# The front of a two-block transformer: x loaded transposed, modulation quarters 2 to 9 as running sums on VectorE, position tables loaded later

## The chip, the cores and the metric

The kernel runs on one core of a Trainium2 chip as one program. The metric is the device time of one execution in microseconds (us), and the median of the runs is quoted. All data are float32.

## The reference

Three transformer blocks run over one sequence of 1024 tokens with 1024 channels. The change lies in the front, the first stage. There the reference computes, for each block, modulation values from a conditioning vector, and for the first block the projection of the modulated tokens:

```
c_act = silu(c)                                   # c is 1 x 1024
mod = c_act @ ada_w[i] + ada_b[i]                 # 1024 x 6144, i = 0, 1; block 3 has w_mod, b_mod and its own c
sh1, sc1, g1, sh2, sc2, g2 = split(mod, 6)
h = x * (1 + sc1) + sh1                           # x is 1024 x 1024
qkv = (h @ w_qkv).reshape(S, 3, 16, 64)           # 1024 x 3072
q = qkv[:, 0] * 64 ** -0.5
```

Neighbourhood attention over q, k, v follows, with a bias table indexed by the distance of the tokens (na_rpb), then the other stages. The front has to deliver q, k and v, all three rows of modulation values (18432 in all), and the spread position tables.

## The kernel before

The front is the function of that name. D = S = 1024, and a matrix of 1024 rows is eight blocks of 128 partitions.

**Quarters and chunks.** The three modulation matrices have 3 x 6144 columns, cut into nine pieces of 2048 columns, called quarters. Only quarter 1 (q = 0 in the code: sh1 and sc1 of the first block) is needed in the front itself; quarters 2 to 9 are written to memory for later stages. A quarter of weights is 8 MB and comes in four chunks of 2 MB. For each chunk TensorE makes a partial sum (partial, L370): for two k and four column groups a matmul with a column of the activated c, spread over 32 columns, as the stationary operand, and 512 columns of weights as the moving one. The four groups lie in four bands of 32 columns of the array and run side by side, and float32 matmuls appear twice in the trace, as two passes. After the fourth chunk VectorE adds the bias to the sum in PSUM (add_row, L478) and POOL stores the row (L352).

**x.** SP loads x by rows into the tile v. TensorE turns it, 64 transposes into PSUM (turn_x, L359), and VectorE and ScalarE copy the results to hT (L432, L446).

**From quarter 1 to h.** When all four chunks of quarter 1 are summed, ScalarE copies the sums to part, four small matmuls turn them into columns (columns, L385), VectorE adds the bias and 1 and multiplies hT in place, eight instructions of 128x1024 (L476).

**Items.** The projection is 48 items (L391) of eight matmuls with 512 moving columns, for six blocks c of 512 weight columns. The blocks of weights (2 MB, L321) lie in two buffers. For c below 4 an item gives 128 columns of q or k, transposed, for half of the tokens; then come the items of v (L407), which are written to the tile v. Four PSUM banks take the items in turn; even items are copied out by VectorE, odd ones by ScalarE. Item n waits until item n - 4 is copied.

**Order.** All of it is written out by hand, as one list per engine. After the items n with n % 3 of 1 or 2 TensorE does one chunk's partial sum (chunk_after): 32 chunks among 48 items. SP is the only queue for large loads and works in order; a chunk's load waits until the chunk two before it is summed (L311).

```
for m in range(FIRST, CHUNKS):
    if m in (12, 17, 22, 28):
        load_weights(2 + (12, 17, 22, 28).index(m))
    load_chunk(m)
```

**POOL** zeroes a table in memory, writes eight shifted copies of the position biases into it and spreads it with 16 more DMAs (L342 to L348), at the start of the program; then it stores the rows of the quarters, and the stage ends when the last store has landed. A barrier of all engines stands between the front and the attention (na in tile names, L531 its first load).

Of the kernel before, what the change touches and what calls it, by code (L numbers as in the profile page):

```python
# [16 lines left out]
P = 128  # L17
# [3 lines left out]
ALU = mybir.AluOpType  # L21
# [4 lines left out]
S = 1024  # L26
# [225 lines left out]
def front(nc, name, a, x, w, mods, table, spread_table, qT, kT, v):  # L252
# [6 lines left out]
    KC, CW, QW, FIRST = D // P, 512, 2048, 4  # L259
    QUARTERS = len(mods) * (6 * D // QW)  # L260
    CHUNKS, ITEMS = 4 * QUARTERS, 48
    H, R, C = a["na_rpb"].shape[1:]
    wv = w.rearrange("(c p) n -> p c n", p=P)
    x_rows = rows(x)
    flat_table = table.rearrange("c h r k -> (c h r k)").rearrange("(p n) -> p n", p=P)
    with Stage(nc, name) as st:
        ident, sel = st.sb("ident", [P, P]), st.sb("sel", [P, 4])
        ccol, cact = st.sb("ccol", [P, 2, KC]), st.sb("cact", [P, 2, KC])
        bcol, col = st.sb("bcol", [P, 2 * KC]), st.sb("col", [P, 2 * KC])
        mw, brow = st.sb("mw", [P, 2, 2, QW]), st.sb("brow", [P, 2, CW])  # L270
# [4 lines left out]
        turn = [st.ps(f"turn{e}", [P, 512]) for e in range(2)]  # L275
        acc = [st.ps(f"acc{e}", [P, 512]) for e in range(4)]
        mp, ms = st.ps("mp", [P, 512]), st.ps("ms", [P, 512])
        id_in, c_in, b_in, act_done = (st.sem(n) for n in ("id_in", "c_in", "b_in", "act_done"))
# [3 lines left out]
        mw_in, brow_in = [st.sem(f"mw_in{j}") for j in range(2)], [st.sem(f"brow_in{j}") for j in range(2)]  # L282
        turned, evac = st.sem("turned"), [st.sem(f"evac{e}") for e in range(2)]
        part_done, part_cp, sum_done, cols_done, h_ready = (st.sem(n) for n in ("part_done", "part_cp", "sum_done", "cols_done", "h_ready"))
        mm_done, mm_cp = st.sem("mm_done"), [st.sem(f"mm_cp{e}") for e in range(2)]
# [8 lines left out]
        def chunk_buffer(m):  # L294
            if m < FIRST:
                return (qT, kT)[m // 2][:, 4 * (m % 2):4 * (m % 2) + 4].rearrange("p a n -> p (a n)").rearrange("p (i n) -> p i n", i=2)
            return mw[:, m % 2]

        def chunk_after(n):

            return FIRST + 2 * (n // 3) + n % 3 - 1 if n % 3 else None
# [2806 lines left out]
```

## Time and profile before

| | before |
|---|---|
| median of 3 runs | 4301.48 us (4300.26 to 4303.33) |
| profiled execution, span | 4301.6 us |
| TensorE busy, whole span | 3568.8 us (83%) |
| VectorE busy, whole span | 1470.4 us (34%) |
| front: first instruction to the next stage's first load | 0.4 to 454.6 us |
| DMA, whole span | 842 MB, mean 196 GB/s |

The profiled execution has a span of 4301.6 us from its first to its last instruction, 0.1 us beside the median of the runs; no other time of that execution is given. PE is TensorE (PEld its weight loads), DVE VectorE, ACT ScalarE, POOL GpSimd, SP the queue of loads. In a timeline a row gives start, duration, engine and line, the operation, output<-inputs, the shape and a count; in brackets stands how long the engine had been idle and for whom. In the view by stretches a row gives, after the limits and the length, the busy us of PE, PEld, DVE, ACT and POOL with their instructions, the granted TensorE clock as a share of full speed, the busy share of the DMA engines and what they moved. In the groups by line a row ends with the busy us, the mean ns of one instruction and the idle time before them. The DMA issues end with the median us from issue to landing.

### The profile page before, as it was taken

What the parts mean: (1) busy time and instruction counts of PE and PEld (TensorE: products, weight loads), DVE (VectorE), ACT (ScalarE), POOL (GpSimd) and SP (SyncE); (2) the same over time, 40 slices, a digit from 0 to 9 for tenths busy, and PEclk for the clock granted to TensorE, in tenths of its full rate; (3) what the DMA queues carried; (4) which work ended last, traced back from release to release, by engine and by line L of the source; (5) the groups of instructions that cost most, each with busy time, mean ns of one, the idle gap of its engine ahead of it and who ended that gap; (6) DMA issues with size and microseconds to landing.
All of it is one profiled execution on the core that took longest, in us unless ns stands there. A gap on an engine that the chain in (4) does not pass through costs nothing. (4 is left out here: it accounts for less than half of the span.)

```text
span 4301.6 us, 49622 instructions
## 1 busy us (share of the span) xinstructions
PE 3568.8 (83%) x19450; PEld 1989.7 (46%) x19450; DVE 1470.4 (34%) x2609; ACT 873.4 (20%) x1883; POOL 242.1 (6%) x277
## 2 busy tenths in 40 slices
PE   7999889479999598999874999986999476929970
PEld 3333555334444244777542444433557374527650
DVE  1000455400000484666452000004426762631116
ACT  0000450001111123555200110102335311001111
POOL 1000200100000010000002000000000000010002
PEclk9999999589999798999986999997999787959995
DMA  8555312099999420000314999955210403129964
GB/s 311 203 201 200 123 57 108 25 389 427 426 424 391 173 84 6 1 2 2 125 64 155 426 426 427 420 217 203 98 51 1 149 3 123 69 64 420 420 272 149
DMA packets 175632, 842.34 MB, mean 196 GB/s; under 512 B 53199, under 2 KB 60111, under 8 KB 129330
## 3 DMA queue, kind: packets, MB, share of 16 engines
q1 hardware_dynamic: 140306, 735.20, 42.6%
q0 software_dynamic: 21856, 58.35, 3.8%
q10 hardware_dynamic: 13248, 45.67, 2.6%
q8 instruction: 158, 2.59, 0.2%
q14 instruction: 64, 0.52, 0.0%
HBM read 758.39 MB, written 97.20 MB: 199 GB/s over the span
## 5 line engine op out<-in xcount | busy, mean ns | idle before, releaser
L403 PE MATMUL front_acc<-front_hT,front_wt 128*128 128x512 f32 x512 | 226.7, 599 | 2.2 <-DMA front_wt<-in_na_w_qkv 2.2
L1238 PE MATMUL n_acc<-n_wt,n_hT 128*128 128x512 f32 (+2 forms) x512 | 191.1, 530 | 0.7 <-ACT n_hT L1278 0.7
L201 DVE TENSOR_REDUCE gqa_top<-gqa_scores 128x1 f32<-128x1024 f32 x128 | 150.8, 1220 | 101.8 <-PE gqa_scores L149 101.8
L232 ACT ACTIVATE gqa_probs<-gqa_scores,gqa_top 128x1024 f32<-128x1024 f32 x128 | 142.5, 1113 | 169.0 <-DVE gqa_top L201 169.0
L2160 PE MATMUL m1x_gp<-m1x_w,m1x_xT 128*128 128x512 f32 (+1 forms) x512 | 172.1, 600 | 1.5 <-issue 0.7
L2160 PE MATMUL m0x_gp<-m0x_w,m0x_xT 128*128 128x512 f32 (+1 forms) x512 | 171.9, 599 | 1.5 <-DVE m0x_xT L2236 0.7
L2185 PE MATMUL m0x_yp<-m0x_w,m0x_hidT 128*128 128x512 f32 (+1 forms) x512 | 169.3, 594 | 2.1 <-ACT m0x_hidT L2246 2.1
L2185 PE MATMUL m1x_yp<-m1x_w,m1x_hidT 128*128 128x512 f32 (+1 forms) x512 | 169.3, 594 | 2.1 <-ACT m1x_hidT L2246 2.1
L2160 PE MATMUL m0x_up<-m0x_w,m0x_xT 128*128 128x512 f32 (+1 forms) x512 | 168.8, 592 | 0.0
L2160 PE MATMUL m1x_up<-m1x_w,m1x_xT 128*128 128x512 f32 (+1 forms) x512 | 168.8, 592 | 0.0
L936 PE MATMUL n_acc<-n_wt,n_hT 128*128 128x512 f32 x384 | 168.0, 597 | 0.7 <-ACT n_hT L954 0.7
L403 PEld LDWEIGHTS front_acc<-front_hT,front_wt 128*128 128x128 f32 x512 | 96.1, 191 | 132.3 <-issue 128.7
L139 PE MATMUL gqa_turn<-gqa_ident,gqa_probs 128*128 128x128 f32 x1024 | 140.4, 281 | 0.1
L139 PEld LDWEIGHTS gqa_turn<-gqa_ident,gqa_probs 128*128 128x128 f32 x1024 | 110.4, 141 | 59.6 <-issue 59.6
L149 PE MATMUL gqa_scores<-k1T,q1T 64*128 64x512 f32 x512 | 131.9, 630 | 5.8 <-DMA gqa_ident<-in_ident 3.3
L1238 PEld LDWEIGHTS n_acc<-n_wt,n_hT 128*128 128x128 f32 x512 | 97.8, 194 | 83.0 <-issue 77.9
L1730 PE MATMUL n_acc<-n_wt,mixT 128*128 128x512 f32 x256 | 114.1, 605 | 15.1 <-DMA n_wt<-in_w_out 15.1
L168 PE MATMUL gqa_out<-gqa_probsT,v 128*64 128x128 f32 x2048 | 125.9, 276 | 0.8 <-ACT gqa_probsT L228 0.8
L1730 PE MATMUL n_acc<-n_wt,o1T 128*128 128x512 f32 x256 | 114.1, 605 | 15.0 <-DMA n_wt<-in_gqa_w_o 15.0
L1730 PE MATMUL n_acc<-n_wt,q0T 128*128 128x512 f32 x256 | 113.7, 604 | 15.2 <-DMA n_wt<-in_na_w_o 15.2
L2300 DVE TENSOR_TENSOR m1x_hid<-m1x_sg,m1x_up 128x512 f32<-128x512 f32 x24 | 16.5, 687 | 321.2 <-PE m1x_up L2160 321.2
L2300 DVE TENSOR_TENSOR m0x_hid<-m0x_sg,m0x_up 128x512 f32<-128x512 f32 x24 | 16.5, 687 | 320.7 <-PE m0x_up L2160 320.7
(612 smaller groups left out, 5529.9 us busy)
## 6 DMA issues: line engine op xcount, KB each, us to landing
m0x_w<-in_moe_w_gate SPq DMA_DIRECT2D x32, 2048.0 KB, 32.8
m0x_w<-in_moe_w_up SPq DMA_DIRECT2D x32, 2048.0 KB, 32.3
m0x_w<-in_moe_w_down SPq DMA_DIRECT2D x32, 2048.0 KB, 33.2
m1x_w<-in_moe_w_gate SPq DMA_DIRECT2D x32, 2048.0 KB, 33.0
m1x_w<-in_moe_w_up SPq DMA_DIRECT2D x32, 2048.0 KB, 31.9
m1x_w<-in_moe_w_down SPq DMA_DIRECT2D x32, 2048.0 KB, 33.4
front_mw<-in_ada_w SPq DMA_DIRECT2D x20, 2048.0 KB, 7.4
m2x_w<-in_moe_w_gate SPq DMA_DIRECT2D x32, 1024.0 KB, 32.2
```

What stands on the lines that cost most here:

```text
L139: last = pe.transpose(turn[f % TURN][:, i * P:(i + 1) * P], src, ident[:, :])
L149: last = pe.matmul(scores[h][:, c * 512:(c + 1) * 512], qT[half, j, t * P:(t + 1) * P], kT[half, 2 * j // SHARE, c * 512:(c + 1) * 512], s ...
L168: pe.matmul(out[h * HEAD:(h + 1) * HEAD, 0:P], v[:, k, kv * HEAD:(kv + 1) * HEAD], probsT[:, n % 2, h, k], start=k == 0, stop=k == TILES - 1)
L201: dve.tensor_reduce(top[:, n % 2, h:h + 1], scores[h][:, :], AX.X, ALU.max, negate=True).then_inc(max_ready, 1)
L232: act.activation(probs[:, n % 2, h], scores[h][:, :], ACT.Exp, bias=top[:, n % 2, h:h + 1], accum_out=total[:, n % 2, h:h + 1]).then_inc(p ...
L403: last = pe.matmul(acc[n % 4][:, :], wt[:, c % 2, k, i * P:(i + 1) * P], hT[:, k, half * 512:(half + 1) * 512], start=k == 0, stop=k == KC ...
L936: last = pe.matmul(acc[t % 2][:, c], hT[:, t % 2, k], wt[:, k, c * 512:(c + 1) * 512], start=k == 0, stop=k == KC - 1)
L1238: last = pe.matmul(acc[c][:, 0:n1 - n0], hT[:, t % 2, k], wt[:, k, n0:n1], start=k == 0, stop=k == KC - 1)
L1730: last = pe.matmul(acc[t % 2][:, c * HALF:(c + 1) * HALF], srcT[:, place(k), t * P:(t + 1) * P], wt[:, k, c * HALF:(c + 1) * HALF], start= ...
L2160: last = pe.matmul(acc[r, 0:F], xT[:, j, k, r], w[:, q % RING, k * F:(k + 1) * F], start=k == 0, stop=k == KC - 1)
L2185: last = pe.matmul(yp[e][r, :], hidT[:, k, r], w[:, q % RING, k * D + e * 512:k * D + (e + 1) * 512], start=k == 0, stop=k == FC - 1)
L2300: dve.tensor_tensor(hid[:, n % 2], sg[:, n % 2], up[n % 2][:, 0:F], ALU.mult).then_inc(hid_done, 1)
```

## The change

x comes from the host already transposed (x_turned), and SP loads it into hT in two halves of the tokens; the 64 transposes and their 16 copies are gone, and the modulation of hT is done in 16 instructions of 128x512, half by half. The first block's items are reordered to match: in each group of eight the four items of the first half of the tokens come first.

Quarter 1 is still summed by TensorE. For quarters 2 to 9 the weights come in steps, eight per quarter, 64 in all: one k of the quarter, 128 x 2048, 1 MB. VectorE multiplies a step by its column of the activated c and adds it to a running sum, total, in SBUF (weigh): a tensor_scalar for the first k, a scalar_tensor_tensor for the other seven. TensorE then adds up the 128 partitions of the running sum with a stationary block of ones, four matmuls per quarter (add_up), after item 4q + 1. VectorE has two steps behind each item's place in its list. The steps lie in a ring of four in the tile v, which is not needed for x any more; items of v wait for the last step. Step s is loaded when step s - 4 is worked off.

POOL starts the position tables when the first item is done (it also sets the block of ones). SP's list begins with the four chunks of quarter 1.

```diff
...
-    KC, CW, QW, FIRST = D // P, 512, 2048, 4
+def front(nc, name, a, w, mods, table, spread_table, qT, kT, v):
+    KC, CW, QW, FIRST, RING = D // P, 512, 2048, 4, 4
     QUARTERS = len(mods) * (6 * D // QW)
-    CHUNKS, ITEMS = 4 * QUARTERS, 48
+    STEPS, ITEMS = KC * (QUARTERS - 1), 48
...
-    x_rows = rows(x)
+    xT = a["x_turned"].rearrange("(c p) s -> p c s", p=P)
...
+        total = st.sb("total", [P, 2, QW])
...
+        mw = v.rearrange("p (s a) n -> p s (a n)", s=RING)
...
+        def place_of(n):
+            return n % 4, n % 8 // 4
...
-                def load_chunk(m):
-                    q, i = m // 4, m % 4
+                def load_step(s):
+                    q, k = s // KC + 1, s % KC
                     weights, bias, _, _ = quarter_of(q)
-                    if m >= FIRST + 2:
-                        sp.wait_ge(part_done, m - 1)
-                    sp.dma_start(chunk_buffer(m), weights[:, 2 * i:2 * i + 2, :]).then_inc(first_in[m] if m < FIRST else mw_in[m % 2], 16)
-                    if q and i == 0:
+                    if s >= RING:
+                        sp.wait_ge(weighed, s - RING + 1)
+                    sp.dma_start(mw[:, s % RING], weights[:, k, :]).then_inc(mw_in[s % RING], 16)
+                    if k == 0:
...
-                sp.dma_start(ident[:, :], a["ident"]).then_inc(id_in, 16)
-                sp.dma_start(sel[:, :], a["mod_sel"]).then_inc(id_in, 16)
-                load_chunk(0)
-                load_chunk(1)
-                sp.dma_start(v[:, 0:4], x_rows[:, 0:4]).then_inc(x_in[0], 16)
-                load_chunk(2)
-                sp.dma_start(v[:, 4:8], x_rows[:, 4:8]).then_inc(x_in[1], 16)
-                load_chunk(3)
+                first = quarter_of(0)[0]
+                for m in range(FIRST):
+                    sp.dma_start(first_buffer(m), first[:, 2 * m:2 * m + 2, :]).then_inc(first_in[m], 16)
+                sp.dma_start(sel[:, :], a["mod_sel"]).then_inc(s_in, 16)
+                sp.dma_start(hT[:, :, 0:512], xT[:, :, 0:512]).then_inc(x_in[0], 16)
                 load_weights(0)
+                sp.dma_start(hT[:, :, 512:S], xT[:, :, 512:S]).then_inc(x_in[1], 16)
+                for s in range(RING):
+                    load_step(s)
                 load_weights(1)
-                for m in range(FIRST, CHUNKS):
-                    if m in (12, 17, 22, 28):
-                        load_weights(2 + (12, 17, 22, 28).index(m))
-                    load_chunk(m)
+                for s in range(RING, STEPS):
+                    if s in (18, 34, 50):
+                        load_weights(2 + (18, 34, 50).index(s))
+                    load_step(s)
+                load_weights(5)
...
+                pool.memset(ones[:, :], 1.0).then_inc(ones_set, 1)
                 pool.memset(zero[:, :], 0.0).then_inc(zeroed, 1)
                 pool.wait_ge(zeroed, 1)
+                pool.wait_ge(mm_done, 1)
                 pool.dma_start(flat_table, zero[:, :]).then_inc(cleared, 16)
...
-                def turn_x(t):
-                    for c in range(2):
-                        f = 2 * t + c
-                        if f >= 2:
-                            pe.wait_ge(evac[f % 2], f // 2)
-                        for i in range(4):
-                            last = pe.transpose(turn[f % 2][:, i * P:(i + 1) * P], v[:, t, (4 * c + i) * P:(4 * c + i + 1) * P], ident[:, :])
-                        last.then_inc(turned, 1)
...
+                def add_up(q):
+                    pe.wait_ge(weighed, KC * q)
+                    if q >= 2:
+                        pe.wait_ge(row_added, q - 1)
+                    for g in range(4):
+                        last = pe.matmul(mp[32 * g:32 * g + 32, :], ones[:, :], total[:, q % 2, g * CW:(g + 1) * CW], start=True, stop=True)
+                    last.then_inc(row_done, 1)
...
+                            i, half = place_of(n)
+                            if c == 0 and i == 0:
+                                pe.wait_ge(h_ready, KC * half + k + 1)
...
-                partial(0)
-                partial(1)
-                pe.wait_ge(x_in[0], 16)
-                for t in range(4):
-                    turn_x(t)
-                partial(2)
-                pe.wait_ge(x_in[1], 16)
-                for t in range(4, TILES):
-                    turn_x(t)
-                partial(3)
+                for m in range(FIRST):
+                    partial(m)
+                pe.wait_ge(s_in, 16)
                 columns()
+                pe.wait_ge(ones_set, 1)
                 for n in range(ITEMS):
                     item(n)
-                    m = chunk_after(n)
-                    if m is not None:
-                        partial(m)
-            def evacuate_x(eng, e, t, copy):
-                f = 2 * t + e
-                eng.wait_ge(turned, f + 1)
-                copy(hT[:, 4 * e:4 * e + 4, t * P:(t + 1) * P], turn[e][:, :].rearrange("p (k s) -> p k s", k=4)).then_inc(evac[e], 1)
+                    if n % 4 == 1 and n > 4:
+                        q = n // 4
+                        if q < QUARTERS:
+                            add_up(q)
...
+                    if n < 34:
+                        eng.wait_ge(weighed, STEPS)
...
-                for t in range(TILES):
-                    evacuate_x(dve, 0, t, dve.tensor_copy)
...
-                for e in range(2):
-                    dve.wait_ge(evac[e], TILES)
-                for k in range(KC):
-                    at = k % 4 * 4 + k // 4
-                    dve.tensor_scalar(hT[:, k], hT[:, k], col[:, at + 2:at + 3], col[:, at:at + 1], ALU.mult, ALU.add).then_inc(h_ready, 1)
+                for half in range(2):
+                    dve.wait_ge(x_in[half], 16)
+                    for k in range(KC):
+                        at = k % 4 * 4 + k // 4
+                        part_of = hT[:, k, half * 512:(half + 1) * 512]
+                        dve.tensor_scalar(part_of, part_of, col[:, at + 2:at + 3], col[:, at:at + 1], ALU.mult, ALU.add).then_inc(h_ready, 1)
+                def weigh(s):
+                    q, k = s // KC + 1, s % KC
+                    by = cact[:, quarter_of(q)[2], k:k + 1]
+                    dve.wait_ge(mw_in[s % RING], 16 * (s // RING + 1))
+                    if k == 0:
+                        if q >= 3:
+                            dve.wait_ge(row_done, q - 2)
+                        dve.tensor_scalar(total[:, q % 2], mw[:, s % RING], by, None, ALU.mult).then_inc(weighed, 1)
+                    else:
+                        dve.wait_ge(weighed, s)
+                        dve.scalar_tensor_tensor(total[:, q % 2], mw[:, s % RING], by, total[:, q % 2], ALU.mult, ALU.add).then_inc(weighed, 1)
...
-                    if m is not None and m % 4 == 3:
-                        add_row(m // 4)
+                    if n % 4 == 2 and 1 <= n // 4 < QUARTERS:
+                        add_row(n // 4)
+                    for s in (2 * n, 2 * n + 1):
+                        if s < STEPS:
+                            weigh(s)
...
+    inputs["x_turned"] = inputs["x"][0].T
...
```

SP at the start of the program, before (v is x there, front_wt the weights of the projection, q0T and k0T hold the chunks of quarter 1):

```order
L323 DMA front_ident<-in_ident 128x128
L324 DMA front_sel<-in_mod_sel 128x4
L312 DMA q0T<-in_ada_w 128x2x2048 x2
L327 DMA v<-in_x 128x4x1024
L312 DMA k0T<-in_ada_w 128x2x2048
L329 DMA v<-in_x 128x4x1024
L312 DMA k0T<-in_ada_w 128x2x2048
L321 DMA front_wt<-in_na_w_qkv 128x8x512 x2
```

and with the change, where v holds the ring of steps:

```order
L323 DMA q0T<-in_ada_w 128x2x2048 x2
L323 DMA k0T<-in_ada_w 128x2x2048 x2
L324 DMA front_sel<-in_mod_sel 128x4
L325 DMA front_hT<-in_x_turned 128x8x512
L319 DMA front_wt<-in_na_w_qkv 128x8x512
L327 DMA front_hT<-in_x_turned 128x8x512
L310 DMA v<-in_ada_w 128x2048
L314 DMA front_brow<-in_ada_b 128x1x512
L310 DMA v<-in_ada_w 128x2048 x3
```

The second half of x and of the weights' blocks now stands behind the first ones; ident is gone, and sel stands behind the chunks.

TensorE at the start, before (front_turn are the transposes, front_ms the columns, front_acc the items, eight matmuls each, front_mp the partial sums):

```order
L382 MATMUL front_mp<-q0T,front_cact 32x512 x16
L365 MATMUL front_turn<-front_ident,v 128x128 x32
L382 MATMUL front_mp<-k0T,front_cact 32x512 x8
L365 MATMUL front_turn<-front_ident,v 128x128 x32
L382 MATMUL front_mp<-k0T,front_cact 32x512 x8
L389 MATMUL front_ms<-front_sel,front_part 128x4 x4
L403 MATMUL front_acc<-front_hT,front_wt 128x512 x16
L382 MATMUL front_mp<-front_mw,front_cact 32x512 x8
L403 MATMUL front_acc<-front_hT,front_wt 128x512 x8
```

and with the change:

```order
L365 MATMUL front_mp<-q0T,front_cact 32x512 x16
L365 MATMUL front_mp<-k0T,front_cact 32x512 x16
L372 MATMUL front_ms<-front_sel,front_part 128x4 x4
L395 MATMUL front_acc<-front_hT,front_wt 128x512 x48
L381 MATMUL front_mp<-front_total,front_ones 32x512 x4
L395 MATMUL front_acc<-front_hT,front_wt 128x512 x32
```

Between the items stand four matmuls on total per 32, where eight stood behind every one or two items.

VectorE from the end of quarter 1 on, before:

```order
L467 TENSOR_TENSOR front_col<-front_ms,front_bcol 128x16
L470 TENSOR_SCALAR front_col<-front_col 128x4x2
L476 TENSOR_SCALAR front_hT<-front_hT,front_col 128x1024 x8
L487 TENSOR_SCALAR q0T<-front_acc 128x512 x3
L483 TENSOR_TENSOR front_row<-front_mp,front_brow 128x512
```

and with the change:

```order
L445 TENSOR_TENSOR front_col<-front_ms,front_bcol 128x16
L448 TENSOR_SCALAR front_col<-front_col 128x4x2
L455 TENSOR_SCALAR front_hT<-front_hT,front_col 128x512 x16
L480 TENSOR_SCALAR q0T<-front_acc 128x512
L465 TENSOR_SCALAR front_total<-v,front_cact 128x2048
L468 SCALAR_TENSOR_TENSOR front_total<-v,front_cact,front_total 128x2048 x3
L480 TENSOR_SCALAR q0T<-front_acc 128x512
L468 SCALAR_TENSOR_TENSOR front_total<-v,front_cact,front_total 128x2048 x4
```

Behind the copy of every even item (L480) there are now four steps, L465 being the first one of a quarter.

## Rows read from the trace of the kernel before

**Rows 1.** Stretch of the partial sums: us, busy per engine, PEclk, DMA share, GB/s.
```profile
66.00:438.00 372.00, 372.00 (x1217) 147.23 (x1216) 20.75 (x30) 13.73 (x23) 3.91 (x7) 1.00 0.53 198
```

**Rows 2.** Timeline of PE: start us, us, engine, line, operation, count.
```profile
66.01 1.92 PE L382 MATMUL front_mp<-front_mw,front_cact 128*32 128x512 f32 x16
67.86 7.13 PE L403 MATMUL front_acc<-front_hT,front_wt 128*128 128x512 f32 x16
74.93 1.92 PE L382 MATMUL front_mp<-front_mw,front_cact 128*32 128x512 f32 x16
76.78 14.00 PE L403 MATMUL front_acc<-front_hT,front_wt 128*128 128x512 f32 x32
90.71 1.92 PE L382 MATMUL front_mp<-front_mw,front_cact 128*32 128x512 f32 x16
```

**Rows 3.** Timeline of PE, before the first items.
```profile
44.76 1.92 PE L382 MATMUL front_mp<-k0T,front_cact 128*32 128x512 f32 x16 [0.60 <-DMA k0T<-in_ada_w]
...
50.69 15.39 PE L403 MATMUL front_acc<-front_hT,front_wt 128*128 128x512 f32 x32 [2.23 <-DMA front_wt<-in_na_w_qkv]
```

**Rows 4.** View by stretches (columns as rows 1), the start.
```profile
0.00:5.00 5.00, 0.00 (x0) 0.00 (x0) 0.00 (x0) 1.50 (x2) 1.60 (x6) 1.00 0.51 111
0.00:35.00 35.00, 13.27 (x80) 6.13 (x80) 2.77 (x4) 3.89 (x6) 14.46 (x30) 0.92 0.94 367
30.00:35.00 5.00, 0.23 (x4) 0.00 (x0) 0.00 (x0) 0.00 (x0) 0.00 (x0) 0.80 1.03 419
45.00:50.00 5.00, 2.74 (x24) 1.23 (x16) 1.36 (x4) 0.60 (x1) 0.00 (x0) 1.00 1.05 393
0.00:50.69 50.69, 23.36 (x136) 13.22 (x136) 7.58 (x13) 6.87 (x11) 14.46 (x30) 0.86 0.97 380
```

**Rows 5.** Timeline of all engines, end of the front.
```profile
445.46 1.92 PE L382 MATMUL front_mp<-front_mw,front_cact 128*32 128x512 f32 x16
445.57 0.60 ACT L446 ACTIVATE v<-front_acc 128x512 f32<-128x512 f32 x1 [15.19 <-PE front_acc L407]
...
447.45 0.69 DVE L483 TENSOR_TENSOR front_row<-front_mp,front_brow 128x512 f32<-128x512 f32 x1 [10.11 <-PE front_mp L382]
448.44 0.55 POOL L352 DMA_DIRECT2D sc_mod<-front_row  x1 [48.86 <-DVE front_row L483]
454.61 0.34 SPq L531 DMA_DIRECT2D na_ident<-in_ident  x1
```

**Rows 6.** DMA issues to 470 us: tensors, queue, count, KB, us to landing.
```profile
front_mw<-in_ada_w SPq DMA_DIRECT2D x20, 2048.0 KB, 7.4
...
front_wt<-in_na_w_qkv SPq DMA_DIRECT2D x6, 2048.0 KB, 16.3
...
sc_rpb_spread<-sc_rpb_table POOLq DMA_DIRECT2D x16, 192.0 KB, 11.2
...
sc_mod<-front_row POOLq DMA_DIRECT2D x8, 8.0 KB, 5.2
```

**Rows 7.** Timeline of DVE, the modulation of hT.
```profile
48.99 5.87 DVE L476 TENSOR_SCALAR front_hT<-front_hT,front_col 128x1024 f32<-128x1024 f32 x8
```

**Rows 8.** Groups by line and form, DVE, whole span: busy us, mean ns, idle.
```profile
L747 DVE SCALAR_TENSOR_TENSOR n_z<-n_y2t,n_gates,n_z 128x1024 f32<-128x1024 f32 x8 | 10.3, 1284 | 1.3 <-DVE n_z L746 1.3
...
L746 DVE TENSOR_SCALAR n_z<-n_yt,n_gates 128x1024 f32<-128x1024 f32 x8 | 6.1, 767 | 17.8 <-DMA n_y2t<-sc_expert_rows,n_idx 13.8 <-DVE n_xn L768 2.6 <-ACT n_rstd L776 1.4
...
L2568 DVE TENSOR_TENSOR gdn_mid<-gdn_mid,gdn_rn 128x2048 f32<-128x2048 f32 x2 | 4.6, 2288 | 0.4 <-ACT gdn_rn L2696 0.4
```

**Rows 9.** Timeline of POOL, its tables' DMA issues.
```profile
1.88 0.68 POOL L342 DMA_DIRECT2D sc_rpb_table<-front_zero  x1 [0.31 <-POOL front_zero L340]
...
19.87 8.29 POOL L348 DMA_DIRECT2D sc_rpb_spread<-sc_rpb_table  x16 [4.48 <-DMA sc_rpb_table<-in_na_rpb]
```

**Rows 10.** Timelines of DVE and of SP, end of the stage behind.
```profile
627.35 0.29 DVE L629 TENSOR_TENSOR q0T<-na_out,na_inv_rows 128x128 f32<-128x128 f32 x1 [0.36 <-ACT na_inv_rows L644]
...
628.45 0.34 SPq L1663 DMA_DIRECT2D n_ident<-in_ident  x1
```

More of the change, by code:

```diff
@@ L273, in front @@
         wt = st.sb("wt", [P, 2, KC, CW])
+        total = st.sb("total", [P, 2, QW])
         zero = st.sb("zero", [P, flat_table.shape[1]])
-        turn = [st.ps(f"turn{e}", [P, 512]) for e in range(2)]
         acc = [st.ps(f"acc{e}", [P, 512]) for e in range(4)]
         mp, ms = st.ps("mp", [P, 512]), st.ps("ms", [P, 512])
-        id_in, c_in, b_in, act_done = (st.sem(n) for n in ("id_in", "c_in", "b_in", "act_done"))
+        s_in, c_in, b_in, act_done, ones_set = (st.sem(n) for n in ("s_in", "c_in", "b_in", "act_done", "ones_set"))
         x_in = [st.sem(f"x_in{j}") for j in range(2)]
@@ L281, in front @@
         first_in = [st.sem(f"first_in{j}") for j in range(FIRST)]
-        mw_in, brow_in = [st.sem(f"mw_in{j}") for j in range(2)], [st.sem(f"brow_in{j}") for j in range(2)]
-        turned, evac = st.sem("turned"), [st.sem(f"evac{e}") for e in range(2)]
+        mw_in, brow_in = [st.sem(f"mw_in{j}") for j in range(RING)], [st.sem(f"brow_in{j}") for j in range(2)]
         part_done, part_cp, sum_done, cols_done, h_ready = (st.sem(n) for n in ("part_done", "part_cp", "sum_done", "cols_done", "h_ready"))
+        weighed, row_done = st.sem("weighed"), st.sem("row_done")
         mm_done, mm_cp = st.sem("mm_done"), [st.sem(f"mm_cp{e}") for e in range(2)]
@@ L358, in _ @@
             def _(pe):
-                def turn_x(t):
-                    for c in range(2):
-                        f = 2 * t + c
-                        if f >= 2:
-                            pe.wait_ge(evac[f % 2], f // 2)
-                        for i in range(4):
-                            last = pe.transpose(turn[f % 2][:, i * P:(i + 1) * P], v[:, t, (4 * c + i) * P:(4 * c + i + 1) * P], ident[:, :])
-                        last.then_inc(turned, 1)
-                def partial(m):
-                    q, i = m // 4, m % 4
-                    which = quarter_of(q)[2]
-                    if m < FIRST:
-                        pe.wait_ge(first_in[m], 16)
-                    else:
-                        pe.wait_ge(mw_in[m % 2], 16 * ((m - FIRST) // 2 + 1))
-                    if i == 0 and q == 1:
-                        pe.wait_ge(part_cp, 1)
-                    elif i == 0 and q:
-                        pe.wait_ge(row_added, q - 1)
+                def partial(m):
+                    pe.wait_ge(first_in[m], 16)
                     for n in range(2):
-                        k = 2 * i + n
+                        k = 2 * m + n
                         for g in range(4):
-                            last = pe.matmul(mp[32 * g:32 * g + 32, :], cact[:, which, k:k + 1].to_broadcast([P, 32]),
-                                             chunk_buffer(m)[:, n, g * CW:(g + 1) * CW], start=k == 0, stop=k == KC - 1)
+                            last = pe.matmul(mp[32 * g:32 * g + 32, :], cact[:, 0, k:k + 1].to_broadcast([P, 32]),
+                                             first_buffer(m)[:, n, g * CW:(g + 1) * CW], start=k == 0, stop=k == KC - 1)
                     last.then_inc(part_done, 1)
@@ L398, in item @@
                     for k in range(KC):
-                        if n == 0:
-                            pe.wait_ge(h_ready, k + 1)
                         if c < 4:
-                            i, half = n % 8 // 2, n % 2
+                            i, half = place_of(n)
+                            if c == 0 and i == 0:
+                                pe.wait_ge(h_ready, KC * half + k + 1)
                             last = pe.matmul(acc[n % 4][:, :], wt[:, c % 2, k, i * P:(i + 1) * P], hT[:, k, half * 512:(half + 1) * 512],
@@ L437, in evacuate_item @@
                 if c < 4:
-                    i, half = n % 8 // 2, n % 2
+                    i, half = place_of(n)
                     dst = (qT if c < 2 else kT)[:, c % 2 * 4 + i, half * 512:(half + 1) * 512]
                 else:
+                    if n < 34:
+                        eng.wait_ge(weighed, STEPS)
                     dst = v[:, n % 8, c % 2 * 512:(c % 2 + 1) * 512]
@@ L451, in _ @@
                 act.activation(cact[:, :, :], ccol[:, :, :], ACT.Silu).then_inc(act_done, 1)
-                for t in range(TILES):
-                    evacuate_x(act, 1, t, copy)
                 act.wait_ge(part_done, FIRST)
@@ L462, in _ @@
             def _(dve):
-                for t in range(TILES):
-                    evacuate_x(dve, 0, t, dve.tensor_copy)
                 dve.wait_ge(b_in, 16)
@@ L483, in add_row @@
                     dve.tensor_tensor(row[:, q % 2], mp[:, :], brow[:, q % 2], ALU.add).then_inc(row_added, 1)
+                dve.wait_ge(act_done, 1)
                 for n in range(ITEMS):
@@ L3035, in build @@
         with nc.sbuf_tensor("k0T", [P, D // P, S], F32) as k0T, nc.sbuf_tensor("v0", [P, TILES, D], F32) as v0:
-            front(nc, "front", a, a["x"][0], a["na_w_qkv"][0],
+            front(nc, "front", a, a["na_w_qkv"][0],
                   [(a["ada_w"][0], a["ada_b"][0:1], 0, mod0), (a["ada_w"][1], a["ada_b"][1:2], 0, mod1), (a["w_mod_2"][0], a["b_mod_2"][0:1], 1, mod2)],
```

17 lines of the change are left out of this document (5 added, 12 removed).

## The prediction

> **What bounds the kernel now.** I read the view by stretches first, then the timeline of PE, then the tail of the stage, and last the prices of single instructions. In the stretch 66 to 438 us TensorE is busy all of its 372 us, at a granted clock of 1.00, while VectorE works 20.8 us and the DMA engines are used 0.53 at 198 GB/s [rows 1]. The front is therefore bound by TensorE, and two other resources have room. What TensorE does there is in its timeline [rows 2]: three items and two partial sums repeat every 90.71 - 66.01 = 24.70 us. An item without a partial sum behind it is the difference 13.93 - 7.07 = 6.86 us (76.78 to 90.71 is two items and one change of weights, 67.86 to 74.93 is one and one change), so three are 20.58 us, and a partial sum of sixteen passes with its changes costs (24.70 - 20.58) / 2 = 2.06 us. The whole stretch closes with these: 48 x 6.86 + 31 x 2.06 + 1.5 = 394.7 us against 445.46 - 50.69 = 394.8. The 1.5 is the start at a low clock: the first two items took 15.39 us instead of 14.00 [rows 3, 2].
>
> Ahead of 50.69 us the stage waits for data: by 35 us 12.8 MB had moved (35 us at 367 GB/s), and the last chunk of quarter 1 came at 44.76 us, behind all of x, the small tables of POOL and three other chunks [rows 3, 4]. Behind 445.46 us the last partial sum, its row and its store hold the barrier until 454.61 us [rows 5].
>
> **Start of the first item.** Chunks are 2.10 MB each. Now 4 chunks, half of x and one block of weights come before the first item needs its last input: 12.6 MB, where it was 14.7 MB and 3.7 MB of POOL's tables (372 + 8 x 22.5 + 16 x 192 KB) [rows 6]. 12.65 MB had moved in the old trace at 34.5 us [rows 4]. The queue begins 0.9 us earlier (two small DMAs are no longer in front), 2 KB rows move at 393 instead of 419 GB/s (4.2 MB, +0.6), and landing comes 1 to 2 us behind the moved bytes (19.3 MB had moved when the weights released PE at 50.69, 18.5 MB had to): 34.5 - 0.9 + 0.6 + 1.5 = 35.7 us. The other inputs are in time: the last chunk at about 24.5 us, then the old chain from chunk to modulation, 48.99 - 44.76 = 4.2 us [rows 3, 7], 29 us; half of x about 30 us; eight modulations of half the width cost at most the old 0.73 us each and run ahead of PE. PE stands still some 8 us before the item, as it did for 2.2 us before, and the old start was already at the low clock, so I keep the 1.5 us. Gain 50.69 - 35.7 = 15.0 us. Bounds: 33 us (no lag) and 42 us (x and weights, 4.2 MB, at the 250 GB/s between the 393 of a full queue and the 111 of its first 5 us). The 64 transposes of x go as well; they lay in waits for DMA, so they are worth nothing of their own.
>
> **Partial sums.** 32 of them leave PE, 31 inside the stretch: 31 x 2.06 = 63.9 us. Eight column sums of 4 matmuls come in. Four matmuls are two groups of passes instead of four; a group is 0.43 us (one item is sixteen), so 2.06 - 0.86 = 1.20 us each, 9.6 us together. Gain 54.3 us. Bounds for one: 0.86 and 2.06 us, 2.7 us better and 6.9 us worse in all.
>
> **What VectorE takes over.** 64 steps of 128x2048. No scalar_tensor_tensor of this width is in the trace. At 1024 columns one with a per-partition scalar takes 1284 ns and a tensor_tensor of 2048 columns takes 2288 ns [rows 8], so I take 2288 + 59 = 2.35 us, with 0.16 us of wait for its own semaphore (1.3 us over 8). The first step of a quarter is a tensor_scalar, 767 ns at 1024 [rows 8], 1.3 us at 2048. For two items VectorE then has four steps, 9.0 to 9.4 us, one copy of 0.69 and half of a row sum, 0.35 us: 10 to 10.5 us in about 13.9. It works them off in one run behind an even item's copy, so the next even copy finds it free about 3.5 us early. Behind it, if it is late, four accumulator banks give two more items before PE stands still. Cost on the path: nothing. The cover fails from (13.9 - 1.7) / 3.5 = 3.5 us per step. A column sum needs the steps of its quarter, which end about 11 us before it is due.
>
> **Loads.** The ring holds four steps of 1.05 MB. Per two items 4.19 MB of steps and a quarter of a block of weights, 0.52 MB, have to come: 345 GB/s with the biases, where the old front asked for 198 and the full queue gave 367 to 393 [rows 1, 4]. A load of 2 MB took 7.4 us from issue to landing [rows 6], four are in flight, and a slot is refilled as soon as its step is done: 7.4 + 2.35 = 9.8 us for four loads, against 13.9. A block of weights lands after 16.3 us, its length in the queue and in 2 KB rows; one in four pairs carries one, and a step behind it may come some us late, which the next pair makes up. The queue is in order, and the waits in front of a block of weights (8, 16, 24 items) fall due in the same run of steps that frees the slot behind it, so nothing extra waits. The start is the tightest place: x's second half, steps 0 to 7, weights and POOL's tables are 16.5 MB behind item 0, about 40 us at 410 GB/s. The copy of item 4 then comes at 77 instead of 71 us, and the PE needs its bank at 93. Cost: nothing.
>
> By the Trainium skill, "DMA: Bandwidth & Descriptors", section "Bandwidth", a transfer of 1 MB reaches only 341 GB/s. The sum would be 12.3 us for four steps by it, about 14.3 us for two items with weights and biases, and a time near 4231 us. The trace of before has no queue of 1 MB loads that would show it; its queued 2 MB loads are faster [rows 4]. It is rival E below.
>
> **POOL** starts its tables only when item 0 is done. They took it from 1.9 us until 28.2, and 11 us more to land [rows 9, 6], so they end near 81 us. The first row store is due at 86 and blocks VectorE only at the third row, near 142 us. Cost: nothing.
>
> **Tail.** With the last row gone by item 34, item 47 is followed by its copy only: 0.11 + 0.60 us [rows 5], and the barrier, 0.8 us from the last VectorE instruction to the next stage's first DMA in the stage behind [rows 10]. 1.5 us instead of 454.61 - 445.46 = 9.15: gain 7.6 us. Everything later hangs on this barrier; no instruction of it changes.
>
> **Sum.** 15.0 + 54.3 + 7.6 = 76.9 us; the next stage starts at 35.7 + 1.5 + 329.3 + 9.6 + 1.5 = 377.6 us instead of 454.61. The profiled execution had a span of 4301.6 us and the median of the runs is 4301.48, so the same gain counts from either: 4224.7, and I say 4225 us.
>
> **The rivals.** (A) The loads do not overlap and bound the front. If each takes half of the measured 7.4 us, alone, two items take 4 x 3.7 + 1.9 = 16.7 us, 2.8 us more in each of 16 pairs: 44 us back, 4269 us. For it: a ring with one step per slot, and a demand that rises from 198 to 345 GB/s. Against it: the queue already streams at 367 to 393 with several loads in it [rows 4]. It works only if the queue loses its overlap altogether. (B) The same place, worse, is the case on the other side: if a 1 MB load costs what a 2 MB load does, 7.4 us, and the next waits for it, two items take 4 x 7.4 + 1.9 = 31.5 us, 16 x 17.6 = 281 us more, 4506 us. It decides from 77 / 16 = 4.8 us over the pace, (13.9 + 4.8 - 1.9) / 4 = 4.2 us per load. Against it is what speaks against A. (C) VectorE is the bound: steps of 2 x 2.35 us, because two operands and a product cost double at this width, give 16 x (16.5 + 1.7 - 13.9) = 69 us back, 4294 us. The row of 1024 columns contradicts it. (D) The change does less than it says: the partial sums go, but x in 2 KB rows and the small tables behind it delay the first item to 42 us and disturb the first pairs by as much again; 4225 + 13 = 4238 us.
>
> (E) Single megabytes stream, but slower than the old loads of two: with 330 GB/s, 10% under the 367 of rows 4, the 4.84 MB of a pair take 14.7 us instead of 13.9, and VectorE hands PE its banks late once the slack of two items is used: 16 x 0.8 = 13 us, 4238 us. For it: nothing but the smaller size; against it: four in flight where the old ring had two. This is the mechanism that the page above speaks of.
>
> **How the numbers follow.** Forecast 0.76 (4214 to 4235: the start -2.5 to +6.5, the column sums -2.7 to +6.9, the barrier +-1); D 0.08; E 0.07; A 0.04; C 0.01; B and anything that makes it slower 0.03; no change 0.01. The range is 4213 to 4244 us: it takes in the bounds, D and E, and leaves out A. A measurement of this kernel can tell 0.2%, 9 us. Faster 0.95, same 0.02, slower 0.03.
>
> **What the profile after would show.** Right: first item's matmul at 34 to 37 us; PE without idle time from there to about 376; column sums some 1.2 us apart from the items; steps of 2.35 us, VectorE near 0.7 busy; DMA share near 0.85; next stage's first DMA near 377. Wrong: PE waiting for a copy of VectorE, and VectorE for a load of a step (A, B, E); steps above 3.5 us (C); a granted clock below 1.00 in the middle of the stage; or the stages behind longer than they were.

## The result, and the profile after

The changed kernel takes 4225.43 us (median of 4 runs, 4223.14 to 4226.01), the kernel before 4301.84 us beside it; the ratio is 0.9823, 95% interval [0.9809, 0.9837]. The profiled execution has a span of 4221.3 us and a time of 4223.1 us. Its page begins:

```profile
span 4221.3 us, 48752 instructions
...
PE 3503.5 (83%) x18938; PEld 1971.7 (47%) x18938; DVE 1605.4 (38%) x2673; ACT 868.7 (21%) x1875; POOL 243.0 (6%) x278
```

TensorE's timeline at the start of the front, against [rows 2, 3]:

```profile
23.52 2.70 PE L365 MATMUL front_mp<-k0T,front_cact 128*32 128x512 f32 x16 [3.09 <-DMA k0T<-in_ada_w]
...
34.47 43.28 PE L395 MATMUL front_acc<-front_hT,front_wt 128*128 128x512 f32 x96 [5.62 <-DMA front_wt<-in_na_w_qkv]
77.68 1.06 PE L381 MATMUL front_mp<-front_total,front_ones 128*32 128x512 f32 x8
78.67 27.73 PE L395 MATMUL front_acc<-front_hT,front_wt 128*128 128x512 f32 x64
106.34 1.06 PE L381 MATMUL front_mp<-front_total,front_ones 128*32 128x512 f32 x8
```

Item 0 begins at 34.47 us instead of 50.69. From one column sum to the next pass 106.34 - 77.68 = 28.66 us; four items are 27.44, so a column sum with its changes of weights costs 1.22 us. The end of the front, all engines, against [rows 5]:

```profile
375.73 0.60 ACT L429 ACTIVATE v<-front_acc 128x512 f32<-128x512 f32 x1 [13.14 <-PE front_acc L399]
377.25 0.33 SPq L526 DMA_DIRECT2D na_ident<-in_ident  x1
```

The last copy ends at 376.33 and the next stage's first load starts at 377.25 us instead of 454.61: 77.4 us of the front are gone. What follows took 3847.0 us before and 3844.1 after; over all kernels here it lies between 3840 and 3849 us without a change in its code. So the single profiles are read below by this mark, the start of the next stage, and the medians stand beside it.

Two resources look different from what the prediction expected. The view by stretches, against [rows 1, 4] (same columns):

```profile
30.00:35.00 5.00, 0.53 (x1) 0.50 (x2) 3.12 (x7) 0.00 (x0) 0.00 (x0) 0.50 1.04 387
35.00:40.00 5.00, 5.00 (x9) 2.04 (x8) 0.00 (x0) 0.00 (x0) 0.00 (x0) 0.68 1.06 399
100.00:260.00 160.00, 160.00 (x405) 68.13 (x404) 111.82 (x65) 6.57 (x11) 3.31 (x6) 1.00 0.99 357
```

The DMA issues of the front, against [rows 6]:

```profile
v<-in_ada_w SPq DMA_DIRECT2D x40, 1024.0 KB, 12.4
...
front_wt<-in_na_w_qkv SPq DMA_DIRECT2D x6, 2048.0 KB, 16.6
...
front_brow<-in_ada_b SPq DMA_DIRECT2D x5, 256.0 KB
...
sc_rpb_spread<-sc_rpb_table POOLq DMA_DIRECT2D x16, 192.0 KB, 12.5
```

VectorE's groups by line in the front (busy us, mean ns, idle before and for whom):

```profile
L468 DVE SCALAR_TENSOR_TENSOR front_total<-v,front_cact,front_total 128x2048 f32<-128x2048 f32 x56 | 131.6, 2351 | 66.0 <-DMA v<-in_ada_w 45.2 <-DMA v<-in_w_mod 17.3
L465 DVE TENSOR_SCALAR front_total<-v,front_cact 128x2048 f32<-128x2048 f32 x8 | 10.2, 1280 | 0.6 <-DMA v<-in_ada_w 0.6
```

A step costs 2351 ns, as forecast from two rows of other shapes, and VectorE is busy 111.8 of 160 us. But the DMA engines are used 0.99, at 357 GB/s only, and VectorE waits some 63 us for steps. One such wait in the timeline of VectorE (L425 and L480 are copies, L465 and L468 the steps):

```profile
124.81 9.71 DVE L468 SCALAR_TENSOR_TENSOR front_total<-v,front_cact,front_total 128x2048 f32<-128x2048 f32 x4
134.44 0.68 DVE L480 TENSOR_SCALAR q0T<-front_acc 128x512 f32<-128x512 f32 x1
135.04 1.28 DVE L465 TENSOR_SCALAR front_total<-v,front_cact 128x2048 f32<-128x2048 f32 x1
140.85 7.28 DVE L468 SCALAR_TENSOR_TENSOR front_total<-v,front_cact,front_total 128x2048 f32<-128x2048 f32 x3 [4.53 <-DMA v<-in_ada_w]
```

The second step of a quarter comes 4.5 us late, and behind it stands a run of three. The last step of quarter 4 (steps 16 to 23) ends at 124.81 + 9.71 = 134.5 us, and TensorE's column sum that needs it starts here:

```profile
135.00 1.06 PE L381 MATMUL front_mp<-front_total,front_ones 128*32 128x512 f32 x8
```

That is 0.5 us of margin. For the eight column sums in turn the margins are 2.1, 2.4, 0.5, 4.7, 3.4, 7.9, 6.6 and 9.6 us. TensorE did not wait, but the chain of loads and steps was just fast enough.

### The profile page after: what moved, and what is told of

It reads as the page before. It is cut to its first block and busy times, and to the rows that moved or that the text cites. A ratio compares the mean times of both kernels' runs of the same rounds, so it can differ in the third digit from the quotient of the medians.

```text
span 4221.3 us, 48752 instructions
## 1 busy us (share of the span) xinstructions
PE 3503.5 (83%) x18938; PEld 1971.7 (47%) x18938; DVE 1605.4 (38%) x2673; ACT 868.7 (21%) x1875; POOL 243.0 (6%) x278
## 5 line engine op out<-in xcount | busy, mean ns | idle before, releaser
L468 DVE SCALAR_TENSOR_TENSOR front_total<-v,front_cact,front_total 128x2048 f32<-128x2048 f32 x56 | 131.6, 2351 | 66.0 <-DMA v<-in_ada_w 45.2
## 6 DMA issues: line engine op xcount, KB each, us to landing
m0x_w<-in_moe_w_gate SPq DMA_DIRECT2D x32, 2048.0 KB, 32.2
```

Source lines behind the costliest of these rows:

```text
L468: dve.scalar_tensor_tensor(total[:, q % 2], mw[:, s % RING], by, total[:, q % 2], ALU.mult, ALU.add).then_inc(weighed, 1)
```

## The experiments

Twelve kernels ran, each beside the kernel before. "Mark" is the start of the next stage's first load in the profile.

### The three gains apart

**x_only**: the kernel before with the changed kernel's start (halves of x, order of loads and items, tables after item 0), the partial sums left on TensorE:

```diff
-                load_chunk(1)
-                sp.dma_start(v[:, 0:4], x_rows[:, 0:4]).then_inc(x_in[0], 16)
...
+                for m in range(FIRST):
+                    load_chunk(m)
+                sp.dma_start(hT[:, :, 0:512], xT[:, :, 0:512]).then_inc(x_in[0], 16)
...
+                    partial(m)
```

> The kernel before with the new start alone: x transposed by halves, chunks of quarter 1 first, items of the first block by halves, position tables after item 0. All partial sums stay on TensorE. My theory (three separate gains that add: start 16.2 us as in the trace after, where item 0 starts at 34.5 instead of 50.7; partial sums 54.3; tail 7.6): item 0 at 34.5 us, next stage's first load at 438.4 instead of 454.6, time 4285 us. Rival (the new start only pays when the partial sums are gone, since chunks 5 to 8 now queue behind x, weights and tables): item 0 at 34.5 but TensorE waits for chunks, gain under 10 us, 4292 us or more.

Measured: 4285.97 us against 4301.37, ratio 0.9962 [0.9948, 0.9975], mark at 439.88 us, 1.5 later than expected. Item 0 starts where it does in the changed kernel:

```profile
34.28 17.08 PE L395 MATMUL front_acc<-front_hT,front_wt 128*128 128x512 f32 x32 [5.46 <-DMA front_wt<-in_na_w_qkv]
```

The start is worth its 15 us alone and the rival falls. 16.4 us are gained up to item 0; two items then take 17.08 us where [rows 3] show 15.39, as the granted clock is still 0.50 from 35 to 40 us, where it is 0.68 in the changed kernel. What the first items lose to the low clock differs from kernel to kernel here, by up to 1.7 us. The rest of the change is 4285.97 - 4225.43 = 60.5 us.

**tail_only**: the kernel before, partial sums three per four items.

```diff
-            return FIRST + 2 * (n // 3) + n % 3 - 1 if n % 3 else None
+            m = FIRST + 3 * (n // 4) + n % 4 - 1
+            return m if n % 4 and m < CHUNKS else None
...
-                    if m in (12, 17, 22, 28):
-                        load_weights(2 + (12, 17, 22, 28).index(m))
+                    if m in (12, 18, 24, 30):
+                        load_weights(2 + (12, 18, 24, 30).index(m))
```

> The kernel before with its partial sums placed three per four items, so that the last one falls after item 42 and not 47. The work of every engine is the same. My theory: the 9.15 us behind the last item shrink to the 1.5 us of a copy and a barrier, and the last partial sum's 2.06 us move into the stretch: next stage's first load at 449.0 instead of 454.6, time 4296 us. Rival (the barrier waits for something else than the store, for instance a queue that has to drain): 454 us unchanged, 4301 us.

Measured: 4294.22 us, ratio 0.9983 [0.9974, 0.9992], mark at 450.53 us. The mark moves by 4.1 us of the 5.6 expected. The rest is at the start and not in the tail: item 0 begins 0.15 us later, at 50.84, and the first two items take 16.66 us instead of 15.39, at a lower clock. Behind the last item the mark comes 1.5 us later, as expected. The median moves by 7.2 us, of which 3.6 lie behind the mark in the single profiles, within the spread of the later stages. The store behind the last row did hold the barrier.

**tables_first**: the changed kernel with POOL's tables at once.

```diff
-                pool.wait_ge(mm_done, 1)
```

> The changed kernel, but POOL's position tables start at once and not after item 0. My theory: 3.7 MB more ahead of item 0 at 400 GB/s, item 0 at 42 to 44 instead of 34.5 us, and everything behind it later by the same 8 us: 4233 us. Rival (the first pairs of items are held up by the tables behind item 0 anyway, so that their place does not matter): item 0 later, but a stretch as much shorter, 4225 us.

Measured: 4234.65 us, 9.2 us more than the changed kernel, mark at 389.34 us.

```profile
45.45 7.05 PE L394 MATMUL front_acc<-front_hT,front_wt 128*128 128x512 f32 x9 [16.13 <-DMA front_wt<-in_na_w_qkv]
```

Item 0 starts 11.0 us later, where 8 to 10 were expected, and the mark comes 12.1 later: nothing is made up. The tables' later place is worth more than half of the start's gain.

### What VectorE and the queue still had to spare

**vector_half_more** and **vector_twice** put a useless instruction in front of seven of eight steps (1024 and 2048 columns):

```diff
+                        dve.scalar_tensor_tensor(spare[:, 0:1024], mw[:, s % RING, 0:1024], by, mw[:, s % RING, 0:1024], ALU.mult, ALU.add)
```

> The changed kernel with one more scalar_tensor_tensor of 128x1024 (1.2 us, result thrown away) in front of seven of eight steps. VectorE then works 1.28 + 7 x (2.41 + 1.23) + 2.07 = 28.8 us per quarter against TensorE's 28.7. My theory (VectorE is covered up to about 3.5 us per step, and loads and steps overlap): 4225 to 4235 us. Rival (VectorE is already at the end of its slack because it waits for loads, so its work adds to the waits): 7 x 1.23 us more per quarter, less the 1.9 us that are free, 8 x 6.7 = 54 us, 4279 us.

> The same with 128x2048 (2.35 us) in front of seven of eight steps: 1.28 + 14 x 2.38 + 2.07 = 36.7 us of VectorE per quarter against 28.7. My theory: VectorE bounds the stage, 8 x 8 = 64 us, less some 10 of slack, 4280 us, and its waits for loads are gone. Rival (work adds to the waits): 8 x (16.5 - 1.9) = 117 us, 4340 us.

Measured: 4236.38 us with the mark at 390.12, 1 us above the expected range, and 4282.27 us with the mark at 436.08. Doubled, the front is 58.8 us longer, and VectorE is busy 157.2 of the 160 us from 100 to 260: it is the bound. With half of it the place of the waits is new. TensorE's timeline at two column sums of vector_half_more:

```profile
112.47 1.93 PE L382 MATMUL front_mp<-front_total,front_ones 128*32 128x512 f32 x8 [5.13 <-DVE front_total L470]
...
144.07 1.06 PE L382 MATMUL front_mp<-front_total,front_ones 128*32 128x512 f32 x8
```

and all its waits for a running sum:

```profile
PE front_mp L382 <- DVE front_total L470: 8.8, 3, 5.1
```

TensorE waits for the column sum's input and not for a bank. The three waits make 8.8 of the 12.9 us that the mark moves. The rest is mostly the clock: behind the wait of 5.1 us four items take 29.80 us instead of 27.73.

**bytes_more**: 256 KB more per step, in rows of 2 KB; VectorE waits for them too.

```diff
+                    sp.dma_start(spare_in[:, s % RING], weights[:, k, 0:512]).then_inc(more_in[s % RING], 16)
```

> The changed kernel with a second load of 128x512 (256 KB, unused) beside each step: 11.8 MB per quarter instead of 9.7. Theory 1 (the queue is full at the 357 GB/s that the trace after shows from 100 to 260 us, DMA share 0.99): 33.1 us per quarter against TensorE's 28.7, 8 x 4.4 = 35 us less 10 to 15 of slack, 4245 to 4250 us. Theory 2 (the queue could give the 410 to 425 of its best stretches, as I took it in the prediction): 28.8 us per quarter, 4225 to 4230 us.

Measured: 4257.88 us, mark at 410.71, and this stretch:

```profile
100.00:260.00 160.00, 148.11 (x364) 62.40 (x363) 95.17 (x55) 5.97 (x10) 2.81 (x5) 0.96 1.00 366
```

At 366 GB/s 11.8 MB take 32.2 us per quarter. The queue is full, which is theory 1, but the time lies above the ranges of both theories: 33 us are lost at the mark, 25.0 of them in four waits for a running sum, so there was no slack of 10 to 15 us.

**loads_of_two**: two steps per load.

```diff
-                    sp.dma_start(mw[:, s % RING], weights[:, k, :]).then_inc(mw_in[s % RING], 16)
+                        sp.dma_start(mw[:, s % RING:s % RING + 2], weights[:, k:k + 2, :]).then_inc(mw_in[s % RING], 16)
```

> The changed kernel with two steps per load, 2 MB, in the same ring (a pair is loaded when the pair before it in its place is worked off). Theory 1 (loads of 1 MB cost rate: 357 GB/s where the old 2 MB loads streamed at 415): rate from 100 to 260 us near 400, VectorE's wait for loads down from 62 to under 40 us, time unchanged, 4225 us. Theory 2 (size is not it, something that comes once per quarter is, such as the bias rows and the weights): rate unchanged or lower, and VectorE waits as long or longer since a slot comes free later; 4225 to 4235 us.

Measured: 4237.73 us, mark at 391.48.

```profile
100.00:260.00 160.00, 151.14 (x370) 64.04 (x369) 102.51 (x58) 5.98 (x10) 3.38 (x6) 0.97 0.89 325
```

The queue is idle more (0.89) and moves hardly more while busy: 325 / 0.89 = 365 GB/s, against 357 / 0.99 = 361. The time is 2.7 us above theory 2's range; the coarse slots cost 12 us. This run alone doesn't acquit the size, since two loads are in flight instead of four. But the kernel before has a stage that queues loads of 1 MB, in the same rows of 8 KB as the steps (m2x_w, 96 loads), and there the queue is full at 420 GB/s:

```profile
3900.00:4100.00 200.00, 199.57 (x1039) 136.02 (x1039) 29.64 (x50) 32.95 (x67) 16.80 (x17) 1.00 1.02 420
```

Size is not the cause; bias_small below agrees, which moves these same 1 MB loads at 396 GB/s while busy.

**bias_small**: the bias only to the four partitions that are stored.

```diff
-                        sp.dma_start(brow[:, q % 2], bias.rearrange("(g n) -> g n", g=4).unsqueeze(1).to_broadcast([4, 32, CW])).then_inc(brow_in[q % 2], 16)
+                        sp.dma_start(brow[0:P:32, q % 2], bias.rearrange("(g n) -> g n", g=4)).then_inc(brow_in[q % 2], 16)
```

> The changed kernel with the bias of a quarter loaded to the four partitions that are stored (8 KB) instead of to all 128 (256 KB); the others hold zero. By bytes this is 3% of a quarter's 9.7 MB, 0.7 us of the queue. Theory 1 (bytes are what counts): VectorE's waits for loads fall from 63 to about 57 us. Theory 2 (rows that are read 32 times over slow the queue by more than their bytes, which is why every quarter's second step comes 4 to 6 us late): they fall below 45 us, and the rate rises from 357 GB/s while the share of busy DMA engines stays. Time 4225 us by both, TensorE being the bound.

Measured: 4223.13 us, mark at 376.82, and the stretch of rate and share:

```profile
100.00:260.00 160.00, 160.00 (x405) 68.08 (x404) 108.44 (x62) 6.58 (x11) 3.31 (x6) 1.00 0.85 337
```

VectorE's waits for loads, here and in the changed kernel:

```profile
DVE front_total L472 <- DMA v<-in_ada_w: 15.8, 11, 4.2
...
DVE front_total L472 <- DMA v<-in_w_mod: 0.8, 1, 0.8
```

```profile
DVE front_total L468 <- DMA v<-in_ada_w: 45.2, 13, 7.8
...
DVE front_total L468 <- DMA v<-in_w_mod: 17.3, 4, 5.5
```

63 us of waits become 17, the share falls from 0.99 to 0.85. This stretch can't price a bias load, since it also moves 3.2 MB less, and the biases are only 1.5 MB of that: its chain is ahead sooner (421 GB/s from 60 to 100 us, against 389). Over the whole front the bytes differ by the eight bias loads alone; here the changed kernel, then bias_small:

```profile
0.00:377.00 377.00, 354.97 (x904) 151.07 (x904) 168.63 (x114) 16.42 (x27) 19.16 (x39) 0.98 0.71 261
```

```profile
0.00:377.00 377.00, 354.48 (x904) 150.17 (x904) 169.71 (x114) 16.61 (x28) 20.10 (x41) 0.99 0.64 255
```

An estimate from these two rows is 0.07 x 377 / 8, about 3 us of the queue per bias load of 0.26 MB, which by its bytes takes 0.7. Theory 2 holds in its waits and fails in its signs: the rate fell and the share did not stay (demand is met: 337 GB/s at 0.85 is 396 while busy). The time is the same, as expected: TensorE is the bound.

bytes_more shows which property of the load costs this. Its 64 added loads have the same size and the same rows of 2 KB, but no load reads a row twice:

```profile
0.00:410.00 410.00, 361.37 (x904) 152.21 (x904) 169.08 (x114) 16.42 (x27) 18.97 (x39) 0.95 0.75 281
```

They add 0.75 x 410 - 0.71 x 377 = 40 us, 0.6 us each. What is left for the bias loads is that each row is read 32 times over.

### Where the loads and TensorE meet

**weights_split**: the first block of weights in two pieces.

```diff
-                load_weights(0)
+                sp.dma_start(wt[:, 0, :, 0:256], wv[:, :, 0:256]).then_inc(w_in[0], 16)
```

> The changed kernel with the first block of weights loaded in two pieces of 256 columns, so that item 0 waits for 1.05 MB less. My theory (the last byte ahead of item 0 sets its start): item 0 at about 32 us instead of 34.5, time 4222.5 us, if rows of 1 KB move as fast as rows of 2 KB. Rival (short rows move slower, or the low clock after the idle time gives it back): item 0 at 34 us or later, 4225 us.

Measured: 4224.36 us, mark at 378.03. Its TensorE timeline:

```profile
32.11 44.24 PE L398 MATMUL front_acc<-front_hT,front_wt 128*128 128x512 f32 x96 [2.76 <-DMA front_wt<-in_na_w_qkv]
77.01 1.07 PE L382 MATMUL front_mp<-front_total,front_ones 128*32 128x512 f32 x8 [0.67 <-DVE front_total L471]
...
135.75 1.07 PE L382 MATMUL front_mp<-front_total,front_ones 128*32 128x512 f32 x8 [1.36 <-DVE front_total L471]
```

Item 0 comes 2.4 us earlier and the gain is gone by the third column sum: 2.0 us go in the two waits, and 1.0 in the first six items, which take 44.24 us instead of 43.28 at a lower clock. So the waits for the running sums, which the expectation had not named, and the rival's low clock each had a part.

**later_half**: vector_half_more with the column sum, row sum and bias two items later.

```diff
-                    if n % 4 == 1 and n > 4:
+                    if n % 4 == 3 and n > 4:
```

> vector_half_more, with each quarter's column sum on TensorE two items later, its row sum on VectorE two items later and its bias rows loaded beside the fifth step and not the first. Engine work and bytes are those of vector_half_more, whose next stage starts at 390.1 us where the changed kernel's starts at 377.3. My theory (the chain of loads and steps is late by up to 15 us from the crowded start on, and the column sum is the first that waits for it, not an accumulator bank): the waits for front_total on PE go, next stage's first load at 378 to 381 us, time about 4227 us. Rival (the chain is simply too slow for TensorE, and any place where they meet waits): the same 12 us appear as waits for banks, 390 us, 4237 us.

Measured: 4222.43 us, mark at 378.25; no wait for front_total on PE is left. 11.9 of the 12.9 us that the added work had cost are back, and the last 1.0 lies in the first items, whose granted clock is 0.50 from 35 to 40 us instead of 0.68. So the banks had room and the column sum had not. The bias loads moved with the sum, but that is not what helps: later_split below moves them too, and VectorE waits 65 us for its steps as in weights_split (46.2 + 19.0 against 45.3 + 20.1).

**later_split** (both edits) and **all_three** (with bias_small):

> weights_split, with column sum, row sum and bias rows later as in later_half. weights_split began item 0 at 32.1 us, 2.4 us earlier than the changed kernel, and gave it back in two waits for the running sums. My theory: without these waits the 2.4 us stay, next stage's first load at 374.9 us instead of 378.0, time 4223 us. Rival (the queue is the bound of the stage, and an earlier start waits elsewhere): 377 to 378 us, 4225 us.

> The changed kernel with the first weights in two pieces, the column sums two items later and the small bias loads. Best version by my theory: item 0 at 32.1 us, no wait of TensorE for VectorE, next stage's first load at 374.9 us, time 4223 us, the size of which is near what a measurement can tell. Rival: as for later_split, 4225 us.

Measured: 4221.16 us, ratio 0.9816 [0.9802, 0.9829], mark at 375.77; and 4222.44 us, 0.9819 [0.9805, 0.9832], mark at 374.91. The marks move by 1.5 and 2.3 us, where 2.4 were forecast for both; the first eight items take 57.96 us in the one and 57.04 in the other, which is the difference. The medians cannot be told from the changed kernel's 0.9823. TensorE waits for no running sum and no bank in either, so the queue is no bound of its own at this pace. What the earlier start is worth in time is not shown: it is smaller than the spread.

## Why the prediction was right, and where it was only just right

- **Start of the first item.** Forecast 35.7 us, measured 34.47. x_only shows that this part stands alone: its time is 15.4 us shorter, forecast 15.0.
- **Partial sums.** Forecast 1.20 us per column sum and 54.3 us in all; measured 1.22 us. From item 0 to the end of item 47 pass 375.6 - 34.5 = 341.1 us, forecast 340.4; before it was 394.8, so 53.7 us are gained.
- **Tail.** Forecast 1.5 us, measured 377.25 - 375.62 = 1.6.
- **Sum.** Front 77.4 us shorter, forecast 76.9; time 4225.4 us, forecast 4225. That the time agrees to 0.4 us is luck, as the stages behind alone vary by 9 us. The rivals A to E did not come.
- **VectorE.** The price of a step was right: forecast 2.35 us, measured 2351 ns. Four in a row take 9.71 us, above the forecast 9.0 to 9.4, which left out the wait between them. The threshold of 3.5 us per step is not confirmed. At 3.6 us the order of the changed kernel loses 12.9 us (vector_half_more), and with the sums two items later 1.0 us (later_half): how much VectorE may take depends on where its sum is due, which the threshold left out.
- **Loads, the step that was mis-sized.** The prediction took the queue to give 367 to 393 GB/s against a demand of 345 and a share of 0.85. It gave 357 at 0.99. The term that was too small is the biases, which the sum counted by their bytes, 0.7 us of the queue each; bias_small puts them at about 3 us. [Rows 1] had a hint of it: 198 GB/s at a share of 0.53 is 374 at full share, where the first 35 us, which hold no bias load, give 367 / 0.94 = 390 [rows 4]. One sign of being wrong did come: VectorE waited for steps, 63 us, though TensorE lost nothing. Rival E named the place (330 GB/s) but blamed the size of the loads. By the Trainium skill, "DMA: Bandwidth & Descriptors", section "Bandwidth", a transfer of 1 MB reaches 341 GB/s; here four in flight gave 396 while busy once the bias rows were small. The prediction says that the trace of before has no queue of 1 MB loads. It has one, the 420 GB/s from 3900 to 4100 us above, and that row speaks against rival E's mechanism.
- **The column sum's margin.** "End about 11 us before it is due" was wrong: it was 2.1, 2.4 and 0.5 us at the first three sums and 9.6 at the last. The start itself went as forecast (the copy of item 4 came at 75.5 us, forecast 77); what the margin left out is that each quarter's steps then wait again for loads. This, not the banks, was the first place to break, in weights_split, vector_half_more, loads_of_two and bytes_more. "Cost: nothing" was right by half a microsecond, which is luck.

Why reading one row 32 times over takes the queue about 3 us is open: the runs show only that neither the bytes nor the short rows do it.

## What to carry to other kernels

Before work is moved off the bound engine, divide the rate of a stretch by its busy share, for each mix of loads: where two stretches differ (374 and 390 GB/s here), ask which load in the mix is slow, and price it apart. Look for queues of the planned kind in all stages, not only in the one that changes. For each consumer of the moved work write down when its input is ready and when it is due, not only for the buffers; a consumer that can wait two items longer at no cost should. A load that is small in bytes can be long in the queue, here one that repeats its source rows.

## What had not been expected of the hardware

A bias load of 256 KB that repeats four rows of 2 KB on 128 partitions occupied the queue for about 3 us (an estimate, 0.26 MB in 3 us is some 90 GB/s), where the other loads of the front moved at 396 GB/s while busy. And the stages behind the front, identical in all kernels, differed by up to 9 us between profiled executions (3840 to 3849), more than the small experiments changed.
